# A shared expert moved ahead of a paired expert loop, and one of two sub-blocks fed to TensorE in two groups of 32 columns

## The chip, the cores and the metric

One core of a Trainium2 chip runs the whole program. The metric is the device time of one execution in microseconds (us); the figure to predict is the median. TensorE does the matrix products, VectorE, ScalarE and GpSimd the rest, and DMA queues move data; the hardware profiler recorded one execution, from which all rows below come.

## What is computed

One layer of an encoder over 2048 tokens of width 1024 in float32: a windowed attention and a pooling branch with a residual, then a mixture of experts with a residual, then an RMS norm. The part the change touches is the mixture:

```python
def swiglu(h, wg, wu, wd):
    return (jax.nn.silu(h @ wg) * (h @ wu)) @ wd
...
    def expert_block(args):
        tok, rw, e = args
        xs = hp[tok]
        y = swiglu(xs, w_gate_e[e], w_up_e[e], w_down_e[e])
        return (y.astype(jnp.float32) * rw[:, None]).astype(hf.dtype)
...
    shared = swiglu(hf, w_sh_gate, w_sh_up, w_sh_down)
    return (routed + shared).reshape(B, S, D)
```

The router takes for each token the sigmoid scores of 128 experts, keeps four of eight groups and in them eight experts, and scales their weights to a sum of 2.5. Every expert and the shared one have gate and up weights of 1024 x 256 and down weights of 256 x 1024, 1 MB each. The router's choice depends on the inputs, so how many tokens an expert gets is known only when the kernel runs. The shared expert takes all 2048 tokens.

## The kernel before

**Token tiles.** `tiles` runs `step(i)` for i from -2 to 17 on every engine: 16 tiles of 128 tokens through norm, input projection, attention, pooling, output projection, second norm and router, each engine handling several tiles in different stages of one step. A step stores the residual x1 (`acc_tab`) and the normed rows h2 (`h2_tab`) in DRAM; SP also stores a tile of zeros into the second half of `acc_tab` (semaphore z_acc). For each token GpSimd scatters eight records (token, weight) into a table `rec_tab` ordered by expert. In it the shared expert stands as the first expert, with all tokens at weight 1 (`shrec`, NSH = 32).

**Index work.** After the last tile VectorE counts each expert's tokens, rounds up to sub-blocks of 64 rows (SUB), and works out for each sub-block its expert, its place in the ring and how many weight loads must have landed. TensorE turns these columns into rows (line 1075), VectorE casts them into `tab`; GpSimd gathers the records, TensorE transposes them (line 1080), and `rec` holds the row numbers of the next units.

**The paired loop.** A unit is two sub-blocks of 64 rows that may belong to different experts. With 32 sub-blocks of the shared expert there were 174 units in the profiled run. Weights arrive in a ring of four slots, one expert each, loaded by SP in expert order (`gate_up`, `down` on the SP side), each when the unit that last used the slot is done. The first sub-block's products read their weights from the ring; for the second VectorE copies gate and up weights to `WBG` (line 886) and ScalarE the down weights to `WBD` (line 603). In one unit b of the loop TensorE does, in this order:

1. the gate and up product of unit b+1 (lines 1089 and 1090): eight k of 128 rows each, and in each k a product with 64 stationary columns for the first sub-block, output partitions 0 to 63, and one for the second, partitions 64 to 127, both 512 columns wide;
2. the first half of the down product of unit b (lines 1096 and 1097), two k;
3. eight transposes of the gathered rows of unit b+2 (line 977) and two of the hidden rows (line 1102);
4. the second half of the down product of unit b.

The stationary operand is a slice of the rows (`xTm`, `hT`), the moving one the weights. ScalarE does silu (594) and copies of transposes (597, 600), VectorE the gated product (892), its copy of transposes (889) and the scaling by routing weight and gate 2 (922), and GpSimd gathers the rows (477) and adds the results into `acc_tab` (511). The shape of a product on the array is in the trace as rows*columns, 128*64 here.

**End.** SP loads both halves of `acc_tab`; VectorE adds them, norms and stores.

Of the kernel before, what the change touches and what calls it, by code (L numbers as in the profile page):

```python
# [6 lines left out]
P = 128  # L7
# [29 lines left out]
NSH = T // SUB  # L37
NUNIT = 256
MAXU = (NSH + T * TOPK // SUB + E) // 2
# [9 lines left out]
            sub=4, after=4, start=4, half=1, shrec=2 * NT, inv=ROT, iotag=NG, tok=NT)  # L49
# [8 lines left out]
def constants():  # L58
# [20 lines left out]
    put("base", (t + 1) * T)  # L79
    sub = np.concatenate([2 * s, 2 * (s + P), 2 * s + 1, 2 * (s + P) + 1], 1)  # L80
    put("sub", sub)
    put("after", sub >= NSH)
    put("start", NSH * (sub >= NSH))
    put("half", (s >= SUB) * (T + P))
    shrec = np.zeros((P, NT, 2), np.int32)
    shrec[:, :, 0] = NT * s + np.arange(NT)[None, :]
    shrec[:, :, 1] = np.float32(1.0).view(np.int32)
    put("shrec", shrec.reshape(P, 2 * NT).view(np.float32))
# [27 lines left out]
def build(nc, A, out):  # L116
# [4 lines left out]
    with ctx:  # L121
# [8 lines left out]
        rec_tab = nc.dram_tensor("rec_tab", [(E + 1) * T + P, 2], i32).ap()  # L130
# [32 lines left out]
        def take(*shape):  # L163
# [80 lines left out]
            s_xin s_xres st_x1 st_h2 st_rec  # L244
            z_acc e_off e_row e_tab e_rec e_rf e_rT v_rec
# [14 lines left out]
        def ok(j):  # L260
            return not isinstance(j, int) or 0 <= j < NT

        def tiles(eng, step, chain=None, per_tile=0):

            for i in range(-2, 2):
                step(i)
            if chain:
                n0 = chain.n
            with eng.Fori(2, 14) as i:
                if chain:  # L270
                    chain.base, chain.n = eng.snap(i * per_tile + (n0 - 2 * per_tile)), 0
                step(i)
                if chain:
                    assert chain.n == per_tile, ("per tile", chain.n)
            if chain:
                chain.base, chain.n = 0, n0 + 12 * per_tile
            for i in range(14, 18):
                step(i)

# [18 lines left out]
        RF = arena[:, 42880:43392].bitcast(i32).rearrange("p (c r a) -> p c r a", c=4, a=2)  # L298
        RFf = arena[:, 42880:43392].rearrange("p (c r a) -> p c r a", c=4, a=2)
        RK = arena[:, 43392:43904].rearrange("p (k n r) -> p k n r", k=2, n=2)  # L300
        RI = over("RI", 2 * NUNIT, 43904, i32)
        RW = over("RW", NUNIT, 44416)
# [13 lines left out]
        def _(sp):  # L316
# [17 lines left out]
            halves = rec_tab[T:(E + 1) * T, :].rearrange("(e h t) a -> h e (t a)", e=E, h=2)  # L334
            for n in range(2):
                sp.dma_start(halves[n], pad_rec).then_inc(s["z_fill"], 16)
            sp.wait_ge(s["c_cst"], 16)
            sp.dma_start(rec_tab[0:T, :].rearrange("(p t) a -> p (t a)", p=P), C("shrec").bitcast(i32)).then_inc(s["z_fill"], 16)
            sp.dma_start(rec_tab[(E + 1) * T:(E + 1) * T + P, :].rearrange("(p t) a -> p (t a)", p=1), pad_rec[0:1, 0:2 * P]).then_inc(s["z_fill"], 16)
# [5 lines left out]
            sp.wait_ge(s["z_fill"], 64)  # L345
# [11 lines left out]
            def step(i):  # L357
# [15 lines left out]
            tiles(sp, step)  # L373

            def gate_up(l, e):
                at = (l + 3) % SLOTS * EW
# [5 lines left out]
            def down(l, e):  # L382
                at = (l + 3) % SLOTS * EW + GUW
# [3 lines left out]
            gate_up(0, None)  # L387
            down(0, None)
            sp.wait_ge(s["p_proj"], NT)
            sp.wait_ge(s["w_g"], 16)  # L390
            sp.wait_ge(s["w_u"], 16)
            gate_up(1, 0)
            sp.wait_ge(s["p_wo"], NT)
            for l in (2, 3):
                sp.wait_ge(s["w_g"], 16 * l)
                sp.wait_ge(s["w_u"], 16 * l)
                gate_up(l, l - 1)
                sp.wait_ge(s["w_d"], 16 * (l - 1))
                down(l - 1, l - 2)

            sp.wait_ge(s["w_g"], 64)
            sp.wait_ge(s["w_u"], 64)
            sp.wait_ge(s["gu_done"], NSH // 2)
            gate_up(4, 3)
            sp.wait_ge(s["w_d"], 48)
            down(3, 2)
            sp.wait_ge(s["e_tab"], 1)
            with sp.Fori(1, E // SLOTS) as q:
                for n in range(SLOTS):
                    e = sp.snap(q * SLOTS + n)  # L410
                    sp.wait_ge(s["w_g"], e * 16 + 16)
# [3 lines left out]
                    u = sp.value_load(tab[0:1, bass.ds(e + (6 * P - 3), 1)], min_val=1, max_val=MAXU)  # L415
                    sp.wait_ge(s["gu_done"], u)
                    settle(sp)
                    gate_up(n + 1, e)
                    sp.wait_ge(s["w_d"], e * 16)
                    settle(sp)  # L420
                    if n == 0:
                        w = sp.value_load(tab[0:1, bass.ds(e + (6 * P - 4), 1)], min_val=1, max_val=MAXU)
                    sp.wait_ge(s["y_done"], w)
                    settle(sp)
                    down(n, e - 1)
                    w = u
            sp.wait_ge(s["w_d"], E * 16)
            u = sp.value_load(tab[0:1, 6 * P + E - 4:6 * P + E - 3], min_val=1, max_val=MAXU)
            sp.wait_ge(s["y_done"], u)
            settle(sp)  # L430
            down(E, E - 1)
# [7 lines left out]
            nu = sp.value_load(nu_i[0:1, 0:1], min_val=NSH // 2 + 1, max_val=MAXU)  # L439
# [15 lines left out]
        def _(g):  # L455
# [16 lines left out]
            g.wait_ge(s["z_fill"], 64)  # L472
# [23 lines left out]
            g.wait_ge(s["z_acc"], 16 * NT)  # L496
            g.wait_ge(s["e_tab"], 1)
            nu = g.value_load(nu_i[0:1, 0:1], min_val=NSH // 2 + 1, max_val=MAXU)
# [20 lines left out]
        def _(act):  # L519
# [8 lines left out]
            def step(i):  # L528
# [24 lines left out]
                if ok(i - 1):  # L553
                    W8(act, "p_h2T", i)
                    A_(h2T[:, 0:4, :], B[2].rearrange("p (a b) -> p a b", a=4), ACT.Copy)
                    A_(h2T[:, 4:8, :], B[3].rearrange("p (a b) -> p a b", a=4), ACT.Copy).then_inc(s["a_h2T"], 1)
# [3 lines left out]
                if ok(i - 1):  # L560
                    W8(act, "p_rt", i)
# [24 lines left out]

            act.wait_ge(s["v_wo"], 1)
            tiles(act, step, ch, ACT_PER_TILE)

            act.wait_ge(s["e_tab"], 1)  # L590
            nu = act.value_load(nu_i[0:1, 0:1], min_val=NSH // 2 + 1, max_val=MAXU)
# [10 lines left out]
            def down_copy(src):  # L602
                nc.scalar.copy(WBD, src).then_inc(s["a_cd"], 1)  # L603
# [3 lines left out]
            act.wait_ge(s["w_d"], 16)  # L607
            down_copy(RING[:, 3 * EW + GUW:4 * EW])
# [6 lines left out]
            with act.Fori(0, MAXU // UNROLL) as q:  # L615
                with act.If(q * UNROLL < nu):
                    for n in range(UNROLL):
                        b = act.snap(q * UNROLL + n)
                        with act.If(b < nu):
                            at = act.value_load(tab[0:1, bass.ds(b + (2 * P + 1), 1)], min_val=0, max_val=(SLOTS - 1) * EW)  # L620
                            need = act.value_load(tab[0:1, bass.ds(b + (4 * P + 1), 1)], min_val=16, max_val=16 * (E + 1))
# [8 lines left out]
                            down_copy(RING[:, bass.ds(act.snap(at + GUW), HALF)])  # L630
# [16 lines left out]
        def _(v):  # L647
# [50 lines left out]
            v.wait_ge(s["z_fill"], 64)  # L698
# [17 lines left out]

            def step(i):
                if ok(i - 1):
# [54 lines left out]
                if ok(i):  # L773
# [4 lines left out]
                    last.then_inc(s["v_yT"], 1)  # L778
                if ok(i - 1):
# [23 lines left out]
                    settle(v)  # L803
                    link(V.max(m8, choice))
# [21 lines left out]
            tiles(v, step, ch, DVE_PER_TILE)  # L826

# [7 lines left out]
            link(V.tensor_tensor_scan(cum, sg[:, 0:E], nsub, float(NSH), ALU.mult, ALU.add))  # L835
# [6 lines left out]
            link(V.tensor_tensor(slot, slot, C("after"), ALU.add))  # L842
            link(V.tensor_tensor(first, first, C("start"), ALU.max))
            link(V.tensor_tensor(first, C("sub"), first, ALU.subtract))
            link(V.scalar_tensor_tensor(out=first, in0=slot, scalar=float(NSH), in1=first, op0=ALU.mult, op1=ALU.add))
            V.tensor_scalar(recb[:, :], first, float((E + 1) * NSH), None, ALU.min).then_inc(s["e_off"], 1)

            link(V.tensor_scalar(lc, slot, float(E), None, ALU.min))
            link(V.tensor_scalar(lq, lc, 0.25, 0.375, ALU.mult, ALU.add))
# [3 lines left out]
            V.tensor_scalar(offf[:, 0:4], lq, 3.0, float(EW), ALU.add, ALU.mult)  # L853
            V.tensor_scalar(offf[:, 4:6], lc[:, 2:4], 16.0, 16.0, ALU.mult, ALU.add)
            link(V.tensor_tensor(sg[:, 0:E], cum, nsub, ALU.subtract))
            link(V.tensor_tensor(sg[:, 0:E], sg[:, 0:E], ident, ALU.mult))
# [7 lines left out]
            V.tensor_copy(nu_i[:, :], units[0:1, :]).then_inc(s["e_off"], 1)  # L864
            v.wait_ge(s["e_row"], 1)
            V.tensor_copy(tab[:, 0:512], B[6][0:1, :])
            V.tensor_copy(tab[:, 512:512 + 3 * P], B[7][0:1, 0:3 * P]).then_inc(s["e_tab"], 1)

# [5 lines left out]
            last_.then_inc(s["e_rf"], 1)  # L874
            v.wait_ge(s["e_rT"], 1)
            V.tensor_copy(RI[:, 0:NUNIT], B[5][:, 0:NUNIT])
            V.tensor_scalar(RI[:, NUNIT:2 * NUNIT], B[5][:, 0:NUNIT], C("half"), None, ALU.add)
            link(V.tensor_copy(RW[:, :], B[5][:, NUNIT:2 * NUNIT]))
# [4 lines left out]
            nu = v.value_load(nu_i[0:1, 0:1], min_val=NSH // 2 + 1, max_val=MAXU)  # L883

            def gu_copy(n, src):
                V.tensor_copy(WBGf[n % 2], src).then_inc(s["v_cg"], 1)  # L886
# [8 lines left out]
            v.wait_ge(s["w_g"], 16)  # L895
            v.wait_ge(s["w_u"], 16)
            v.wait_ge(s["st_x1"], 16 * NT)
            gu_copy(0, RING[:, 3 * EW:3 * EW + GUW])
# [268 lines left out]
```

## Time and profile before

| | us |
|---|---|
| median of 2 runs | 3126.52 (3125.52 to 3127.51) |
| the profiled execution | 3141.75 |
| its span, first to last instruction | 3139.7 |
| TensorE products busy | 2849.2 (91%) |
| TensorE weight loads busy (beside products) | 1231.1 (39%) |
| VectorE busy | 1466.8 (47%) |
| ScalarE busy | 852.9 (27%) |
| GpSimd busy | 788.4 (25%) |

### The profile page before, as it was taken

The page shows a single profiled execution, that of the slowest core. Times are in us where ns is not written, and L with a number is a line of the kernel's source. Part 1 is how long each engine was busy: PE and PEld are TensorE (multiplying, and loading weights), DVE is VectorE, ACT ScalarE, POOL GpSimd, SP SyncE. Part 2 cuts the span into 40 slices and gives each one's busy share as a digit, 9 for nine tenths or more (in the row PEclk, how much of TensorE's full clock was granted, in tenths as well). Part 3 has the DMA queues.
Part 4 walks back from the last instruction along what each step waited for, and adds up shares of the span by engine and source line. Part 5 has one row for each costly group of instructions (what it writes and reads, how often), then busy time and mean ns, then how long its engine had stood idle before and what let it go on. Part 6 is the DMA issues. An engine that isn't in the chain of part 4 may idle for free.

```text
span 3139.7 us, 48012 instructions
## 1 busy us (share of the span) xinstructions
PE 2849.2 (91%) x13408; PEld 1231.1 (39%) x13409; DVE 1466.8 (47%) x2449; ACT 852.9 (27%) x1285; POOL 788.4 (25%) x493
## 2 busy tenths in 40 slices
PE   6789898898963999999999999999999999999990
PEld 2355545545541333333333333333333333333330
DVE  1146676666764444444444444444444444444345
ACT  0033333333320222222222222222222222222224
POOL 0000101111113333333332332333233333233220
PEclk9899999999986999999999999999999999999995
DMA  9611111211114347678999999899999996979958
GB/s 374 200 54 47 54 63 37 67 47 54 61 42 183 81 91 240 200 208 248 311 310 351 350 314 346 267 314 308 346 311 312 305 345 199 312 222 313 362 148 327
DMA packets 150957, 684.89 MB, mean 218 GB/s; under 512 B 26577, under 2 KB 27218, under 8 KB 101010
## 3 DMA queue, kind: packets, MB, share of 16 engines
q1 hardware_dynamic: 95730, 516.34, 41.3%
q0 software_dynamic: 55200, 168.21, 24.9%
q8 instruction: 14, 0.23, 0.0%
q14 instruction: 13, 0.11, 0.0%
HBM read 574.22 MB, written 128.07 MB: 224 GB/s over the span
## 4 chain that ended last, share of the span: by engine, by line
PE 61%; DMA 5%; DVE 1%; SPq 1%; issue 1%; POOL 0%; ACT 0%; DVEq 0%; POOLq 0%; ACTq 0%
PE PB L1089 36%; PE PB L1096 18%; PE PB L977 5%; DMA arena<-in_w_up_e 3%; PE PB L1102 1%; DMA arena<-acc_tab 1%; PE PB L1090 1%; DVE arena L954 0%; DVE arena L940 0%; SPq L415 0%; PE PB L1097 0%; DMA acc_tab<-arena,rec 0%; DMA arena<-h_tab,rec 0%; SPq L379 0%; SPq L446 0%
## 5 line engine op out<-in xcount | busy, mean ns | idle before, releaser
L1089 PE MATMUL PB<-arena 128*64 (+1 forms) x2800 | 1232.0, 593 | 2.1 <-issue 1.2
L1090 PE MATMUL PB<-arena 128*64 128x512 f32 x2800 | 1232.1, 593 | 0.0
L511 POOL DMA_INDIRECT acc_tab<-arena,rec x174 | 465.7, 2676 | 1361.8 <-DVE arena L922 1288.4
L1089 PEld LDWEIGHTS PB<-arena 128*64 128x64 f32 x2800 | 383.9, 137 | 802.4 <-issue 802.4
L1096 PE MATMUL PB<-arena 128*64 x1392 | 664.2, 599 | 0.0
L1097 PE MATMUL PB<-arena 128*64 128x512 f32 x1392 | 664.2, 599 | 0.0
L886 DVE COPY arena<-arena 128x4096 f32 (+1 forms) x177 | 405.0, 2288 | 59.9 <-DMA arena<-in_w_up_e 58.9
L922 DVE SCALAR_TENSOR_TENSOR arena<-PB,RW,G 128x512 f32<-128x512 f32 x348 | 245.3, 747 | 299.5 <-PE PB L1097 267.0
L1090 PEld LDWEIGHTS PB<-arena 128*64 128x64 f32 x2800 | 383.9, 137 | 0.0
L892 DVE TENSOR_TENSOR arena<-arena,PB 128x256 f32<-128x256 f32 x175 | 106.7, 610 | 543.4 <-ACT arena L594 541.3
L469 POOL DMA_INDIRECT rec_tab<-recs,posi x128 | 124.0, 969 | 849.3 <-DVE recs L758 809.4
L603 ACT COPY arena<-arena 128x2048 f32 (+1 forms) x175 | 330.9, 1891 | 0.0
L1096 PEld LDWEIGHTS PB<-arena 128*64 128x64 f32 x1392 | 176.6, 137 | 328.0 <-issue 328.0
L594 ACT ACTIVATE arena<-PB 128x256 f32<-128x256 f32 x175 | 67.1, 383 | 826.4 <-PE PB L1090 756.0
L977 PE MATMUL PB<-cst,arena 128*128 128x128 f32 x1664 | 231.4, 283 | 63.0 <-DVE arena L824 34.9
L1007 PE MATMUL PB<-arena 128*128 128x512 f32 (+1 forms) x768 | 280.2, 525 | 1.7 <-ACT arena L532 1.2
L977 PEld LDWEIGHTS PB<-cst,arena 128*128 128x128 f32 x1664 | 183.2, 142 | 217.8 <-issue 159.6
L889 DVE COPY arena<-PB 128x512 f32<-128x512 f32 x176 | 121.7, 691 | 291.8 <-PE PB L977 291.8
L1066 PE MATMUL PB<-arena 128*128 128x512 f32 x512 | 238.6, 627 | 9.6 <-ACT arena L571 6.8
L597 ACT ACTIVATE arena<-PB 128x512 f32<-128x512 f32 x176 | 105.4, 599 | 462.6 <-PE PB L977 462.6
L477 POOL DMA_INDIRECT arena<-h_tab,rec x178 | 187.8, 1055 | 62.5 <-issue 54.0
L1007 PEld LDWEIGHTS PB<-arena 128*128 128x128 f32 x768 | 145.2, 191 | 131.9 <-issue 120.6
(228 smaller groups left out, 1905.4 us busy)
## 6 DMA issues: line engine op xcount, KB each, us to landing
arena<-in_w_gate_e SPq DMA_DIRECT2D x128, 1024.0 KB
arena<-in_w_up_e SPq DMA_DIRECT2D x128, 1024.0 KB
arena<-in_w_down_e SPq DMA_DIRECT2D x128, 1024.0 KB
arena<-in_ada_w SPq DMA_DIRECT2D x12, 2048.0 KB, 13.0
arena<-in_x SPq DMA_DIRECT2D x32, 512.0 KB, 4.3
acc_tab<-arena SPq DMA_DIRECT2D x32, 512.0 KB, 5.0
arena<-acc_tab SPq DMA_DIRECT2D x6, 2048.0 KB, 22.2
h_tab<-arena SPq DMA_DIRECT2D x16, 512.0 KB, 2.9
```

The costliest lines, as they stand in the source:

```text
L477: g.indirect_dma_start(xg[n % AHEAD], None, h2_tab, bass.IndirectOffsetOnAxis(ap=rec[:, n % UNROLL, 0:1], axis=0), bounds_check=T - 1, oob ...
L511: g.indirect_dma_start(acc_tab, bass.IndirectOffsetOnAxis(ap=rec[:, n, 1:2], axis=0), ys[n % 2], None, compute_op=ALU.add).then_inc(s["add ...
L603: nc.scalar.copy(WBD, src).then_inc(s["a_cd"], 1)
L886: V.tensor_copy(WBGf[n % 2], src).then_inc(s["v_cg"], 1)
L922: last_ = V.scalar_tensor_tensor(out=ys[n % 2][:, c * 512:(c + 1) * 512], in0=B[4 + c], scalar=RW[:, bass.ds(b, 1)], in1=G2[:, c * 512:(c ...
L977: last = tr(B[banks[k // 4]][:, (k % 4) * P:(k % 4 + 1) * P], src[:, k * P:(k + 1) * P], ident)
L1007: last = mm(B[4 + n][:, 0:w], xT[:, k, :], w_in[:, k, n * 512:n * 512 + w], start=(k == 0), stop=(k == KD - 1))
L1066: last = mm(B[4 + n], mixT[:, k, :], w_out[:, k, n * 512:(n + 1) * 512], start=(k == 0), stop=(k == KD - 1))
L1089: mm(B[7][0:SUB, :], xTm[:, k, 0:SUB], wa(k), start=(k == 0), stop=(k == KD - 1))
L1090: last = mm(B[7][SUB:P, :], xTm[:, k, SUB:P], WBG[n % 2][:, k], start=(k == 0), stop=(k == KD - 1))
L1096: mm(B[4 + c][0:SUB, :], hT[:, k, 0:SUB], wa(k), start=(k == 0), stop=(k == 1))
L1097: last = mm(B[4 + c][SUB:P, :], hT[:, k, SUB:P], WBD[:, k * D + c * 512:k * D + (c + 1) * 512], start=(k == 0), stop=(k == 1))
```

## The change

**Shared expert.** It leaves the table of records, the counts and the loop (NSH, `shrec`, `after`, `start` go; MAXU is lower by 16; the ring's slot of expert e becomes e mod 4). Its weights are loaded into slot 3 before the token tiles begin, three SP issues ahead of `tiles(sp, step)`. In each tile SP now stores the transposed rows h2T in a new table `hT_tab` in place of the zeros, and ScalarE waits, before it overwrites h2T, for the store of the tile before. From the last token tiles on, `shared(j)` on each engine handles 16 tiles of 128 rows: SP loads the transposed rows into one of three buffers, TensorE does eight k of gate/up with all 128 stationary columns (half before and half after the two hidden transposes of the tile before) and the four down products of the tile before, ScalarE silu and a copy, VectorE the gated product and two products by gate 2, and SP stores the result as the second half of `acc_tab`. These tiles are written into the order of the router and index work: tile 0 after step 15 and tile 1 inside step 16 on TensorE, 2 and 3 before step 17, 4 to 7 before the row work, 8 to 11 before the transposes of the records, 12 to 15 after them. The first gathered rows are transposed between the hidden rows and the down product of tile 15. GpSimd waits for all 16 stores (sh_st) before its first scatter. The first units take weights from the ring through `tab` as all others.

**Second sub-block.** Its products are cut in two groups of 32 stationary columns, with output partitions 64 to 95 and 96 to 127, each over the same 512 moving columns as before.

```diff
-NSH = T // SUB
-MAXU = (NSH + T * TOPK // SUB + E) // 2
+RPE = T // SUB
+MINU = E // 2
+MAXU = (T * TOPK // SUB + E) // 2
...
-                if ok(i):
-                    sp.dma_start(acc_tab[bass.ds(i * P + (T + P), P), :], zeros).then_inc(s["z_acc"], 16)
+                if ok(i - 1):
+                    W8(sp, "a_h2T", i)
+                    sp.dma_start(rows(hT_tab, i - 1), h2T.rearrange("p k n -> p (k n)")).then_inc(s["st_hT"], 16)
...
+            gate_up(3, None)
+            down(3, None)
+            tiles(sp, step, between={NT - 1: first_rows})
             sp.wait_ge(s["p_proj"], NT)
-            gate_up(1, 0)
...
+            gate_up_after(0, 0)
+            down_after(0, 0)
+            for j in range(NT):
+                if j + 3 < NT:
+                    sp.wait_ge(s["sh_gu"], j + 1)
+                    shared_rows(j + 3)
...
+                sp.wait_ge(s["sh_ys"], j + 1)
+                W8(sp, "sh_st", 16 * j)
+                sp.dma_start(acc_tab[T + P + j * P:T + P + (j + 1) * P, :], yss[j % 2]).then_inc(s["sh_st"], 16)
+
+            sp.wait_ge(s["sh_y"], NT)
+            gate_up_after(3, 3)
+            down_after(3, 3)
...
-            g.wait_ge(s["z_acc"], 16 * NT)
+            g.wait_ge(s["sh_st"], 16 * NT)
...
                     W8(act, "p_h2T", i)
+                    W8(act, "st_hT", 16 * (i - 1))
...
+            def shared_gate_up(j, ks):
+                bank = B[0 if j % 2 else 7]
+                for k in ks:
+                    last = mm(bank, xTs[j % 3][:, k, :], gu_view(arena[:, 3 * EW + k * F:3 * EW + k * F + GUW]), start=(k == 0), stop=(k == KD - 1))
+                return last
...
+            def shared(j):
+                shared_begin(j)
+                if j:
+                    shared_hidden(j - 1)
+                shared_end(j)
+                if j:
+                    shared_down(j - 1)
...
-            tiles(pe, step)
-
+            tiles(pe, step, between={NT - 1: shared_first, NT: shared_next})
+
+            for j in range(4, 8):
+                shared(j)
             pe.wait_ge(s["e_off"], 2)
...
+            for j in range(12, NT):
+                shared(j)
+            shared_hidden(NT - 1)
+            pe.wait_ge(s["v_rec"], 1)
+            pe.wait_ge(s["xg_r0"], 16)
+            transposes((2, 3), xg[0], "xg_used")
+            shared_down(NT - 1)
...
                 for k in range(KD):
                     mm(B[7][0:SUB, :], xTm[:, k, 0:SUB], wa(k), start=(k == 0), stop=(k == KD - 1))
-                    last = mm(B[7][SUB:P, :], xTm[:, k, SUB:P], WBG[n % 2][:, k], start=(k == 0), stop=(k == KD - 1))
+                    for r in (slice(SUB, 96), slice(96, P)):
+                        last = mm(B[7][r, :], xTm[:, k, r], WBG[n % 2][:, k], start=(k == 0), stop=(k == KD - 1), tile_position=(0, r.start))
                 last.then_inc(s["gu_done"], 1)
...
                 for k in range(2):
                     mm(B[4 + c][0:SUB, :], hT[:, k, 0:SUB], wa(k), start=(k == 0), stop=(k == 1))
-                    last = mm(B[4 + c][SUB:P, :], hT[:, k, SUB:P], WBD[:, k * D + c * 512:k * D + (c + 1) * 512], start=(k == 0), stop=(k == 1))
+                    for r in (slice(SUB, 96), slice(96, P)):
+                        last = mm(B[4 + c][r, :], hT[:, k, r], WBD[:, k * D + c * 512:k * D + (c + 1) * 512], start=(k == 0), stop=(k == 1), tile_position=(0, r.start))
                 return last
```

## Rows read from the trace of the kernel before

**Rows 1.** Table of stretches: stretch, its length, busy (count) per engine, clock, DMA share, GB/s.

```profile
150.00:170.00 20.00, 9.66 (x43) 6.65 (x43) 4.25 (x11) 6.89 (x16) 0.00 (x0) 0.78 0.07 18
928.00:1000.00 72.00, 12.38 (x52) 9.07 (x52) 37.59 (x114) 5.67 (x10) 28.49 (x25) 0.58 0.53 196
1012.00:2852.00 1840.00, 1839.67 (x9124) 697.50 (x9126) 783.90 (x943) 495.00 (x628) 584.14 (x313) 1.00 0.84 272
2852.00:2992.00 140.00, 130.80 (x642) 49.26 (x640) 55.18 (x67) 34.69 (x44) 36.49 (x23) 0.96 1.01 351
```

**Rows 2.** TensorE's timeline within a unit: start us, duration us, line, tile, count.

```profile
1802.71 0.59 PE L1097 MATMUL PB<-arena 128*64 128x512 f32 x1
...
1803.99 0.59 PE L1096 MATMUL PB<-arena 128*64 x1
1804.00 0.59 PE L1097 MATMUL PB<-arena 128*64 128x512 f32 x1
1804.52 1.09 PE L977 MATMUL PB<-cst,arena 128*128 128x128 f32 x8
1805.45 0.38 PE L1102 MATMUL PB<-cst,arena 128*128 128x128 f32 x2
1805.76 0.64 PE L1096 MATMUL PB<-arena 128*64 x1
...
1806.24 0.59 PE L1096 MATMUL PB<-arena 128*64 x1
...
1816.21 1.09 PE L977 MATMUL PB<-cst,arena 128*128 128x128 f32 x8
```

**Rows 3.** The page's costliest groups: count, busy us, mean ns of one, idle before.

```profile
L1089 PE MATMUL PB<-arena 128*64 (+1 forms) x2800 | 1232.0, 593 | 2.1 <-issue 1.2
L1089 PEld LDWEIGHTS PB<-arena 128*64 128x64 f32 x2800 | 383.9, 137 | 802.4 <-issue 802.4
L1096 PE MATMUL PB<-arena 128*64 x1392 | 664.2, 599 | 0.0
L886 DVE COPY arena<-arena 128x4096 f32 (+1 forms) x177 | 405.0, 2288 | 59.9 <-DMA arena<-in_w_up_e 58.9
L922 DVE SCALAR_TENSOR_TENSOR arena<-PB,RW,G 128x512 f32<-128x512 f32 x348 | 245.3, 747 | 299.5 <-PE PB L1097 267.0
L892 DVE TENSOR_TENSOR arena<-arena,PB 128x256 f32<-128x256 f32 x175 | 106.7, 610 | 543.4 <-ACT arena L594 541.3
L603 ACT COPY arena<-arena 128x2048 f32 (+1 forms) x175 | 330.9, 1891 | 0.0
L594 ACT ACTIVATE arena<-PB 128x256 f32<-128x256 f32 x175 | 67.1, 383 | 826.4 <-PE PB L1090 756.0
```

**Rows 4.** TensorE's timeline from the last token tile to the loop, and the loop's end.

```profile
924.65 3.17 PE L1066 MATMUL PB<-arena 128*128 128x512 f32 x7
...
939.08 1.97 PE L977 MATMUL PB<-cst,arena 128*128 128x128 f32 x8 [11.15 <-DVE arena L740]
...
1000.66 1.08 PE L1089 MATMUL PB<-arena 128*64 128x512 f32 x1 [0.88 <-DVE arena L889]
...
1009.46 1.09 PE L977 MATMUL PB<-cst,arena 128*128 128x128 f32 x8
...
1012.33 0.64 PE L1089 MATMUL PB<-arena 128*64 x1 [1.25 <-issue]
...
3057.57 0.59 PE L1096 MATMUL PB<-arena 128*64 x1
```

**Rows 5.** TensorE's timeline in a token tile: the scores, and the attention product.

```profile
600.22 1.59 PE L991 MATMUL PB<-arena 64*64 64x128 f32 x32
601.75 0.23 PE L998 MATMUL PB<-c 128*128 128x128 bf16 x1
...
626.87 1.09 PE L1043 MATMUL PB<-arena 128*64 128x256 f32 x8 [1.32 <-issue]
627.89 0.38 PE L1047 MATMUL PB<-arena,poolw 128*128 128x128 f32 x1
```

More of the change, by code:

```diff
@@ L48 @@
 COLS = dict(ident=P, band0=NPG * P, band=NPG * P, bandp=NPG * P, tri=P, iota=P, base=P,
-            sub=4, after=4, start=4, half=1, shrec=2 * NT, inv=ROT, iotag=NG, tok=NT)
+            sub=4, half=1, inv=ROT, iotag=NG, tok=NT)
 AT = {}
@@ L261, in ok, with tiles @@
             return not isinstance(j, int) or 0 <= j < NT
-        def tiles(eng, step, chain=None, per_tile=0):
+        def tiles(eng, step, chain=None, per_tile=0, between={}):
             for i in range(-2, 2):
@@ L278, in tiles @@
                 step(i)
+                if i in between:
+                    between[i]()
         def rows(table, i):
@@ L778, in step @@
                     last.then_inc(s["v_yT"], 1)
+                if last_tile:
+                    shared_gated(0)
+                    shared(1)
                 if ok(i - 1):
@@ L803, in step @@
                     settle(v)
+                    if last_tile:
+                        shared(2)
                     link(V.max(m8, choice))
@@ L824, in step @@
                     V.tensor_tensor(xn, xn, B1, ALU.add).then_inc(s["v_xn"], 1)
-            tiles(v, step, ch, DVE_PER_TILE)
+            tiles(v, step, ch, DVE_PER_TILE, between={NT: lambda: shared(3)})
+            shared(4)
             cnt, nsub, cum, le = rk, scores, choice, repl
@@ L893, in gated @@
                                 B[7][:, F:2 * F].rearrange("t (p k) -> t p k", k=2), ALU.mult).then_inc(s["h_ready"], 1)
[L895 to L898, printed above, removed]
+            shared(12)
+            gu_copy(0, 0)
+            for j in range(13, NT):
+                shared(j)
             v.wait_ge(s["xg_used"], 1)
             rows_lower()
-            gu_copy(1, RING[:, 3 * EW:3 * EW + GUW])
+            v.wait_ge(s["sh_hp"], NT)
+            gu_copy(1, 1)
+            shared_out(NT - 1)
             v.wait_ge(s["eg_done"], 1)
@@ L1025, in step @@
                 if ok(i - 1):
+                    if isinstance(i, int) and i == NT:
+                        shared(1)
                     W8(pe, "a_h2T", i)
@@ L1070, in _ @@
             pe.wait_ge(s["c_win"], 16)
-            tiles(pe, step)
+            tiles(pe, step, between={NT - 1: shared_first, NT: shared_next})
+            for j in range(4, 8):
+                shared(j)
             pe.wait_ge(s["e_off"], 2)
             for c in range(NTABS):
-                row = mm(B[6 + c // 4][0:1, (c % 4) * P:(c % 4 + 1) * P], offf[:, c:c + 1], ident, start=True, stop=True)
+                row = mm(B[6 if c < 4 else 3][0:1, (c % 4) * P:(c % 4 + 1) * P], offf[:, c:c + 1], ident, start=True, stop=True)
             row.then_inc(s["e_row"], 1)
+            for j in range(8, 12):
+                shared(j)
             pe.wait_ge(s["e_rf"], 1)
```

259 lines of the change are left out of this document (159 added, 100 removed).

## The prediction

> **What bounds the kernel now.** I read the page first, for the busy shares and the costliest groups, then a table of stretches, then TensorE's timeline inside one unit of the paired loop and between the token tiles and that loop. The reader is to see four things.
>
> First, the paired loop is the program: TensorE is busy for 1839.67 of the 1840 us from 1012 to 2852 at the full clock of 2.4 GHz (1.00 in the table), and afterwards starves a little (130.80 of 140) where the DMA share is 1.01 [rows 1]. Second, a unit lasts 11.69 us, from the transposes at 1804.52 to those at 1816.21 [rows 2]. Each fp32 product runs as two passes (175 gate/up sets of eight products give 2800 passes per sub-block, 174 down sets give 1392 [rows 3]), a pass of 512 columns takes 0.43 us (1802.71 to 1804.00 is three), and the passes of the two sub-blocks start within 0.01 us of each other [rows 2]. So 48 passes cost the time of 24. Third, VectorE (2288 + 2 x 747 + 610 ns and one copy of some 0.7, about 5 us a unit) and ScalarE (1891 + 383 ns and two more short copies, about 3.3 us) fit in 11.69 us with room [rows 3]. Fourth, between the last token tile (seven passes from 924.65, the last streamed by 927.65) and the first gate/up at 1000.66 [rows 4], TensorE is busy for 12.4 of 72 us, at a granted clock of 0.58, and waits for VectorE and DMA otherwise [rows 1].
>
> **The change, part by part.** The loop's bodies run from 1012.33 to the last pass, 3057.57 plus 0.43 [rows 4]: 2045.7 us for 174 units, of which 174 x 11.69 = 2034.1 is the unit and 11.6 is starving.
>
> *The shared expert leaves the loop.* Its 32 sub-blocks of 64 rows were 16 units, so 158 units stay. It comes back as 16 tiles of 128 rows with full-width products: 24 passes and 2 transposes each. A full-width pass also takes 0.43 us (seven merged in 3.17 us, of which the last is 0.59: six steps of 0.43 [rows 4]), so a tile is 24 x 0.4287 + 2 x 0.11 = 10.51 us, and 16 are 168.2 us. A unit of the shared expert was 11.69, so the array time saved is only 16 x 1.18 = 19 us; the rest of the gain is that these tiles fill the hole before 1000.66. TensorE from 927.65: 168.2, plus 4.6 waiting for the last tile's h2 (shared tile 0 ends at 934.5, the transposes can start at 939.08 [rows 4]), plus 6 to 12 for the router, table and row work that is there today (12.4 at today's clock of 0.58, about half at full clock [rows 1]), plus 1.4 for the last hidden rows' trip through ScalarE and VectorE. The first gate/up starts near 1109 instead of 1000.66, and the first body near 1119 instead of 1012.33, since today's first set runs partly at a lower clock (8.8 us) and waits 1.25 us after it [rows 4]. I take **+107 us**; bounds 105 (no waits) and 125 (each of the 16 tiles waits 1 us for a hand-over of 0.38 + 0.61 us [rows 3]).
>
> What this hides costs nothing: VectorE's 16 x (0.61 + 2 x 0.75) = 34 us [rows 3] and its index work (37.6 us busy today [rows 1]) lie beside 180 us of TensorE; the router chain comes about 10 us later, beside shared products. The shared weights (three SP issues of 1 MB) move ahead of the tile loop's input rows in SP's queue; the DMA share from 150 to 170 is 0.07 [rows 1], so they have landed before anyone waits; without that cover they cost some 9 us at the 351 GB/s of the busiest stretch [rows 1]. The zero fill of the second accumulator half becomes a store of h2T of the same 512 KB in each tile; ScalarE's new wait for that store is for one issued a whole token tile earlier, and behind it wait the h2T copy and TensorE's router product. Row loads and result stores of the shared tiles, 1 MB per 10.5 us, go beside the loads of experts 0 to 2. Expert 3's weights are asked for only when the shared tiles are done; they are wanted some units later, and GpSimd's first scatter waits for the last result store, which has a whole unit. If all of this were exposed I would not get over 20 us.
>
> *The second sub-block in two groups of 32 columns.* Call the groups A (columns 0 to 63), B and C (64 to 95, 96 to 127). The order is A, B, C for each k. No row shows a 32-wide group beside a 64-wide one, so this is bounded from both sides.
>
> What rows do show is how TensorE treats tiles. In the attention product (line 1043) the order in the program is two instructions for the one column half, then two for the other, yet 8 passes of 256 columns (0.214 us each) start at 626.87 and are followed at 627.89, that is four passes' time and 0.16: an instruction for another tile of the same shape overtakes waiting ones. The scores (line 991) do 32 passes of 128 columns (0.107 us) in 1.53 us, less than 16 x 0.107 = 1.71, so more than two tiles ran at once there [rows 5]. But between shapes it is different: from 128*64 to 128*128 the last pass starts at 1804.00 and the next shape at 1804.52, 0.09 after the 0.43 it streams; back again, two transposes of 0.11 (eight take 0.93 with the change before them) start at 1805.45 and the next shape at 1805.76, again 0.09; and the first pass after each change takes 0.48, not 0.43 [rows 2]. So a change of shape ends all overlap, its weights aren't loaded ahead, and it costs 0.09 + 0.05 = **0.14 us**. Check: 24 x 0.4287 + 10 x 0.11 + 2 x 0.14 = 11.67, against 11.69.
>
> If 64 and 32 columns are two shapes in this sense, A runs alone for two passes, then B and C together for two. A unit then has 48 passes' time (20.58), ten transposes 1.10, and 25 changes (A to BC and back for each of twelve k, one more for the transposes): 25 x 0.14 = 3.50. Sum **25.2 us**, against 11.69. The first gate/up takes 16 us for 7. If the changes of width cost nothing but the turn, the unit is 20.58 + 1.10 + 0.28 = 22.0. If a change waits for the recorded end of a pass (0.59 less 0.43) and then for a whole weight load of 0.13 (weight loads of 128*64 average 137 ns [rows 3]), it costs 0.29 and the unit 28.9. I take 25.2, because the same step is seen twice in each unit. TensorE would wait for nothing else, and the 11.6 us of starving go, as an expert's 3 MB gets twice the time.
>
> On the one side stands the Trainium skill, "TensorEngine Tiling (Array Packing)", section "Key Properties": changing the tiling mode, not just the tile, drains TensorE, and its list has 128x64 and 128x32 as two modes; by it the sum is the one below. By that rule, the trace agrees as far as it goes: the 0.09 us gaps. On the other, "TensorE: Matmul & The Clock Gate", section "The mechanism", addresses the array in 32-column strips by mask and lets different positions overlap; by it the sum is that of the first rival.
>
> **Sum.** The profiled run took 3141.75 us (span 3139.7); the median is 3126.52, 15 lower, and I carry that over. 3126.5 + 107 + 9 (first gate/up) + 158 x 25.18 (3978.4) - 2045.7 = **5175 us**. The two bounds of the change give 3126.5 + 107 + 7 + 158 x 21.96 - 2045.7 = 4665 and 3126.5 + 107 + 11 + 158 x 28.9 - 2045.7 = 5765; the start's bound adds 18 at most.
>
> **The rivals.**
> 1. *Three groups at once; the width is no change of shape.* Groups that touch different columns don't conflict, and [rows 5] show more than two tiles at once. Then the unit stays 11.69 and the starving stays: 3126.5 + 107 + 158 x 11.69 + 11.6 - 2045.7 = **3046 us**, 2.6% faster. It decides as soon as one pass of B starts within a pass of A. The second page named above speaks for it. Against it: every change of shape in the trace drained, though each there was between tiles that share columns, so the rows can't exclude it. Chance 0.14, of which 0.03 that waits in the 16 shared tiles keep it above 3064.
> 2. *Two at once.* The array takes any two groups: three passes' time per pair, unit 12 x 1.286 + 1.38 = 16.8, 3126.5 + 107 + 4 + 2654 - 2045.7 = 3846 us. The scores speak against it [rows 5]. 0.02.
> 3. *B and C one after the other too*, since they read the same columns of weights: unit 72 x 0.4287 + 1.10 + 3.50 = 35.5, about 6810 us. Same-shape overlap speaks against it. 0.02.
> 4. *The clock falls to 1.2 GHz* in the loop, as half of the columns idle: passes of 0.86 us, unit near 47 us, about 8640 us. The clock was 0.96 where TensorE was busy for 130.80 of 140 us [rows 1]; streaming would be 82% of the new unit. 0.02.
>
> **How the numbers follow.** The likeliest is taking turns, 0.80, at 5175 us with 4660 to 5765 as its range; that already holds 8 in 10, so the other cases stay out of the range. A difference under 2% is about what can't be told from no change. Faster by over 2%: 0.11 (rival 1). Within 2%: 0.03. Slower: 0.80 + 0.06 = 0.86.
>
> **What would show it.** First set of shared products from 927.7 on without holes over 5 us, and the first gate/up near 1109; 158 units. In a unit: passes of A with none of B or C beside them, B and C within 0.01 us of each other, steps of 0.48 and 0.52 us by turns, 2.0 us per k in the gate/up. TensorE busy throughout, no idle for weights. I am wrong if a pass of 32 columns starts while one of 64 streams, if a change costs far from 0.14 us, or if the granted clock in the loop falls below 1.00.

## The result and the profile after

The changed kernel takes 5154.72 us (median of two runs, 5153.79 to 5155.65) where the kernel before takes 3126.52: a ratio of 1.648, with an interval of 1.645 to 1.651. The forecast was 5175, in a range of 4660 to 5765.

First the page of the changed kernel: busy time and share of each engine, the granted clock of TensorE in 40 slices, the instruction queue (packets, MB, share), and the costliest groups.

```profile
PE 4943.8 (96%) x16704; PEld 1342.3 (26%) x16705; DVE 1430.5 (28%) x2398; ACT 818.1 (16%) x1255; POOL 818.4 (16%) x461
...
PEclk9899999999999999999999999999999999999996
...
q8 instruction: 19, 0.31, 0.0%
...
L1220 PE MATMUL PB<-arena 128*64 x2544 | 1363.9, 618 | 1.1 <-DVE arena L961 1.1
L1222 PE MATMUL PB<-arena 128*32 128x512 f32 x5088 | 1338.3, 605 | 0.0
...
L1228 PE MATMUL PB<-arena 128*64 x1264 | 677.7, 618 | 0.0
L1230 PE MATMUL PB<-arena 128*32 128x512 f32 x2528 | 664.9, 605 | 0.0
```

The gate/up passes of the first sub-block (L1220) and of the two groups of the second (L1222) are busy for 1364 and 1338 us. In the kernel before, the passes of the two sub-blocks lay on top of each other and the group of one of them had 1232 us in all [rows 3]; here the two lines add up. Their idle time is 1.1 and 0.0 us: nothing is waited for. VectorE is busy for 28% of the span and ScalarE for 16%, so the loop is TensorE's alone.

One unit on TensorE (start us, duration us, line, tile, count; passes that overlap or follow at once are merged into one line):

```profile
3005.25 1.07 PE L1228 MATMUL PB<-arena 128*64 x2
3006.25 1.05 PE L1230 MATMUL PB<-arena 128*32 128x512 f32 x4
3007.23 1.07 PE L1228 MATMUL PB<-arena 128*64 x2
3008.23 1.05 PE L1230 MATMUL PB<-arena 128*32 128x512 f32 x4
3009.22 1.09 PE L1094 MATMUL PB<-cst,arena 128*128 128x128 f32 x8
3010.15 0.38 PE L1235 MATMUL PB<-cst,arena 128*128 128x128 f32 x2
3010.46 1.07 PE L1228 MATMUL PB<-arena 128*64 x2
```

Two passes of the 64-wide group run alone, then four of the 32-wide ones in the time of two, then the next two of the 64-wide: 1.00 and 0.98 us by turns, 1.98 us for a k. [rows 2] had the same k of both sub-blocks in 0.86 us. The distances between single records, which the rows above merge, say where it goes. Within a turn of the 64-wide group the second pass starts 0.480 us after the first, and the first 32-wide pass 0.523 after that, which is 0.429 of streaming (the step between passes of one width, as in [rows 2]) and 0.094 of nothing. Within a turn of the 32-wide groups the step is 0.453, and the two groups start 0.007 us apart; the next 64-wide pass starts 0.522 after the later of them. From 1130 to 5050 us no pass of one width starts less than 0.521 us after the last one of the other.

From the last token tile to the loop, also on TensorE:

```profile
909.13 7.03 PE L1048 MATMUL PB<-arena 128*128 128x512 f32 x16
...
920.26 1.97 PE L1094 MATMUL PB<-cst,arena 128*128 128x128 f32 x8 [3.99 <-DVE arena L798]
...
1091.11 1.07 PE L1220 MATMUL PB<-arena 128*64 x2
...
1106.99 1.09 PE L1094 MATMUL PB<-cst,arena 128*128 128x128 f32 x8
...
1109.71 1.07 PE L1220 MATMUL PB<-arena 128*64 x2 [1.09 <-DVE arena L961]
...
5068.55 1.05 PE L1230 MATMUL PB<-arena 128*32 128x512 f32 x4
```

The shared tiles begin at 909.13, where the last token tile ends, have one hole of 3.99 us and a small one of 0.38, and the first gate/up of the loop follows at 1091.11. The first body starts at 1109.71, where it was 1012.33 [rows 4]. From there to the end of the last pass at 5069.4 (its start, 5069.0, plus 0.43) are 3959.7 us, 158 units of 25.06; before, it was 2045.7 for 174.

The table of stretches (length, busy and count of each engine, clock, DMA share, GB/s):

```profile
928.00:1110.00 182.00, 180.43 (x493) 78.78 (x492) 61.21 (x145) 18.21 (x39) 26.91 (x25) 1.00 0.45 162
1130.00:5050.00 3920.00, 3920.00 (x12830) 797.80 (x12828) 796.44 (x941) 494.43 (x627) 673.58 (x313) 1.00 0.44 137
150.00:170.00 20.00, 10.12 (x35) 5.87 (x33) 3.84 (x11) 6.50 (x15) 0.00 (x0) 0.86 0.34 140
```

Where [rows 1] had TensorE busy for 12.38 of 72 us at a clock of 0.58, it is busy for 180.43 of 182 at 1.00. In the loop it never waits, at 2.4 GHz throughout, with a DMA share of 0.44.

### The profile page after: what moved, and what is told of

It reads as the page before. It is cut to its first block, busy times and chain, and to the rows that moved or that the text cites. A ratio compares the mean times of both kernels' runs of the same rounds, so it can differ in the third digit from the quotient of the medians.

```text
span 5151.8 us, 53361 instructions
## 1 busy us (share of the span) xinstructions
PE 4943.8 (96%) x16704; PEld 1342.3 (26%) x16705; DVE 1430.5 (28%) x2398; ACT 818.1 (16%) x1255; POOL 818.4 (16%) x461
## 4 chain that ended last, share of the span: by engine, by line
PE 91%; DVE 5%; DMA 2%; ACT 1%; issue 1%; SPq 0%; DVEq 0%; ACTq 0%; POOLq 0%
PE PB L1220 25%; PE PB L1222 24%; PE PB L1228 12%; PE PB L1230 12%; PE PB L1124 6%; PE PB L1094 4%; PE PB L1048 2%; PE PB L1040 1%; PE PB L1071 1%; DMA arena<-in_ada_b 1%; PE PB L1185 1%; PE PB L1235 1%; PE PB L1151 1%; PE PB L1108 1%; DMA arena<-acc_tab 0%
## 5 line engine op out<-in xcount | busy, mean ns | idle before, releaser
L1220 PE MATMUL PB<-arena 128*64 x2544 | 1363.9, 618 | 1.1 <-DVE arena L961 1.1
L1222 PE MATMUL PB<-arena 128*32 128x512 f32 x5088 | 1338.3, 605 | 0.0
L528 POOL DMA_INDIRECT acc_tab<-arena,rec x158 | 515.6, 3263 | 3250.6 <-DVE arena L994 3080.6
L1228 PE MATMUL PB<-arena 128*64 x1264 | 677.7, 618 | 0.0
L1230 PE MATMUL PB<-arena 128*32 128x512 f32 x2528 | 664.9, 605 | 0.0
L964 DVE TENSOR_TENSOR arena<-arena,PB 128x256 f32<-128x256 f32 x159 | 96.3, 606 | 1802.8 <-ACT arena L632 1802.7
L1220 PEld LDWEIGHTS PB<-arena 128*64 128x64 f32 x2544 | 243.1, 134 | 1066.7 <-issue 1066.7
L1222 PEld LDWEIGHTS PB<-arena 128*32 128x32 f32 x5088 | 183.5, 108 | 1032.0 <-issue 1032.0
L958 DVE COPY arena<-arena 128x4096 f32 x161 | 369.5, 2295 | 147.5 <-issue 76.8
L994 DVE SCALAR_TENSOR_TENSOR arena<-PB,RW,G 128x512 f32<-128x512 f32 x316 | 222.7, 746 | 601.0 <-PE PB L1230 601.0
L641 ACT COPY arena<-arena 128x2048 f32 x159 | 300.5, 1890 | 0.7 <-issue 0.7
L1094 PE MATMUL PB<-cst,arena 128*128 128x128 f32 x1536 | 213.5, 283 | 66.1 <-DVE arena L887 53.2
L1228 PEld LDWEIGHTS PB<-arena 128*64 128x64 f32 x1264 | 120.8, 134 | 423.8 <-issue 423.8
L1230 PEld LDWEIGHTS PB<-arena 128*32 128x32 f32 x2528 | 91.2, 108 | 512.8 <-issue 512.8
L494 POOL DMA_INDIRECT arena<-h_tab,rec x162 | 167.9, 1037 | 158.3 <-issue 94.3
```

The source lines that it names most:

```text
L494: g.indirect_dma_start(xg[n % AHEAD], None, h2_tab, bass.IndirectOffsetOnAxis(ap=rec[:, n % UNROLL, 0:1], axis=0), bounds_check=T - 1, oob ...
L528: g.indirect_dma_start(acc_tab, bass.IndirectOffsetOnAxis(ap=rec[:, n, 1:2], axis=0), ys[n % 2], None, compute_op=ALU.add).then_inc(s["add ...
L641: nc.scalar.copy(WBD, RING[:, bass.ds(act.snap(at + GUW), HALF)]).then_inc(s["a_cd"], 1)
L958: V.tensor_copy(WBGf[n % 2], RING[:, bass.ds(at, GUW)]).then_inc(s["v_cg"], 1)
L994: last_ = V.scalar_tensor_tensor(out=ys[n % 2][:, c * 512:(c + 1) * 512], in0=B[4 + c], scalar=RW[:, bass.ds(b, 1)], in1=G2[:, c * 512:(c ...
L1094: last = tr(B[banks[k // 4]][:, (k % 4) * P:(k % 4 + 1) * P], src[:, k * P:(k + 1) * P], ident)
```

## The experiments

My theory was that the 64-wide and the 32-wide groups take turns because TensorE drains at each change of tile shape, and that all of the loss lies there. The rivals: that the *number* of groups costs (three matmuls where two were), that the change of shape costs only its gaps and not the overlap, and that the move of the shared expert has a part in the loss. The chips of these runs give the kernel before 3147 to 3148 us, 21 more than the first; so I go by the ratios.

**The parts apart: e1_shared_only and e2_split_only.** The first keeps the shared tiles and puts the second sub-block back into one group of 64 columns (in the down products the same):

```diff
-                    for r in (slice(SUB, 96), slice(96, P)):
-                        last = mm(B[7][r, :], xTm[:, k, r], WBG[n % 2][:, k], ..., tile_position=(0, r.start))
+                    last = mm(B[7][SUB:P, :], xTm[:, k, SUB:P], WBG[n % 2][:, k], ...)
```

> The changed kernel with the second sub-block's products as one group of 64 columns again; only the shared expert's move is left. Theory (two additive parts): a unit is back at 11.69 us, 158 of them, with the loop's first body some 100 us later after the last token tile than in the kernel before (193.7 less 8.9 of the first split gate/up, against 84.7), and the starving on weights near the loop's end is back: 3126.5 + 100 - 16 x 11.69 = 3040 us, ratio to before 0.972. Rival A (the slowdown is partly the shared tiles' own, for instance through the ring's new start): the unit stays above 12 us and the time above 3200. Rival B (the shared tiles gain nothing because they only move work): 3110 to 3140.

The second is the kernel before with the two `for r` loops alone.

> The kernel before with only the second sub-block split in two groups of 32 columns. Theory (a change of shape drains the array, 25.07 us a unit as in the changed kernel): 3126.5 + 9 + 174 x 25.07 - 2045.7 = 5452 us, ratio 1.744. Rival (the parts interact, the split costs less where the shared tiles are in the loop): the 16 shared units differ from the others, and the total is off by over 50 us.

Measured: e2 takes 5469.4 us, ratio 1.737 (1.733 to 1.741), and all its 174 units have the same form and last 25.06 us. It adds 2322 us to the kernel before, where I had expected 2325. So the split alone makes the loss, and it makes it in the kernel before as in the changed one. TensorE in e2:

```profile
2000.92 0.38 PE L1104 MATMUL PB<-cst,arena 128*128 128x128 f32 x2
2001.23 1.07 PE L1097 MATMUL PB<-arena 128*64 x2
2002.23 1.05 PE L1099 MATMUL PB<-arena 128*32 128x512 f32 x4
2003.21 1.07 PE L1097 MATMUL PB<-arena 128*64 x2
```

e1 missed its expectation: 3149.3 us, ratio 1.001 (0.998 to 1.003), where I had expected 0.972. The move of the shared expert takes 16 units out of the loop and gives no time. The median unit is 11.69 us, and the stretch ahead of the loop is 106 us longer than before, where I had expected some 100. But ten units, from transposes to transposes, last 12.8 to 24.3 us, and all units together take 85.6 us more than 158 medians; in the kernel before it was 10.6. TensorE stands still for 64 of the 85.6 us, and the rest are passes at a lower granted clock behind the holes (0.98 over the whole loop). Where I speak of starving, in the expectations too, it is this sum. One of those holes in e1, on TensorE:

```profile
2868.35 1.09 PE L1094 MATMUL PB<-cst,arena 128*128 128x128 f32 x8
2879.86 0.69 PE L1233 MATMUL PB<-cst,arena 128*128 128x128 f32 x2 [10.42 <-DVE arena L964]
```

And the weight loads that SP issues in e1 around it (start, duration, queue, line, out<-in):

```profile
2859.99 0.33 SPq L386 DMA_DIRECT2D arena<-in_w_down_e  x1
2863.91 0.34 SPq L380 DMA_DIRECT2D arena<-in_w_gate_e  x1
2864.35 0.38 SPq L381 DMA_DIRECT2D arena<-in_w_up_e  x1
2884.28 0.33 SPq L386 DMA_DIRECT2D arena<-in_w_down_e  x1
2885.77 0.33 SPq L380 DMA_DIRECT2D arena<-in_w_gate_e  x1
```

The chain of work behind that hole (start, duration, what):

```profile
2864.35 12.44 DMA arena<-in_w_up_e
...
2879.22 0.60 DVE arena L964
```

The hole ends with the up weights asked for at 2864.35: VectorE's copy of them starts at 2877.01, after 15.35 us of waiting for this load, and the gated product L964, which TensorE needs, comes behind the copy. So that load was asked for too late. And while TensorE waits SP asks for nothing: after down, gate and up the next issue comes 20 us later, once TensorE goes on. The changed kernel does not only renumber the ring's slots. It also rewrites the order on SP: behind the gate and up of expert e comes the down of the same expert, which waits for `y_done` of the last unit that used the slot (expert e - 4), and that product comes behind the gate/up of the next unit; the kernel before put the down of e - 1 there, which waits for a product one expert further back. Every gate and up behind it in SP's queue waits with it. My part-by-part list had gone over SP's queue in the start only.

**The load order: e6_down_behind and e8_before_own_down.** e6 is e1 with the order of the kernel before, the down of e - 1 behind the gate and up of e (in short form):

```diff
                     gate_up(n, e)
-                    sp.wait_ge(s["w_d"], e * 16 + 16)
-                    sp.wait_ge(s["y_done"], u)
-                    down(n, e)
+                    sp.wait_ge(s["w_d"], e * 16)
+                    sp.wait_ge(s["y_done"], w)
+                    down((n - 1) % SLOTS, e - 1)
```

> The kernel with the shared expert moved and no split (e1), and SP's order of weight loads as in the kernel before: the down weights of an expert are asked for after the gate and up weights of the next one, so that the wait for the last unit's y_done holds nothing up. In e1 the units starved for 85.6 us in all, in the kernel before for 10.6. Theory (SP's wait for y_done ahead of the next expert's gate and up weights causes it): starving falls back to 10 to 20 us and the time by some 70 us, ratio to before 0.975 to 0.98. Rival (the head start is missing: the kernel before fills four slots during 16 shared units): starving stays above 60 us and the ratio near 1.00.

e8 is the kernel before with nothing but the other order:

```diff
-                    sp.wait_ge(s["w_d"], e * 16)
+                    sp.wait_ge(s["w_d"], e * 16 + 16)
...
-                    sp.wait_ge(s["y_done"], w)
-                    down(n, e - 1)
+                    sp.wait_ge(s["y_done"], u)
+                    down(n + 1, e)
```

> The kernel before, with only SP's order of loads changed to the changed kernel's: each expert's down weights right behind its own gate and up weights, with the wait for y_done of the slot's last unit between. Theory (this order causes the starving): starving rises from 10.6 to some 80 us, time 70 us above the kernel before, ratio 1.02. Rival (missing head start): no change, ratio 1.00.

Measured: e6 takes 3077.55 us, ratio **0.977** (0.975 to 0.979), faster than both kernels; e8 3227.7, ratio 1.025 (1.024 to 1.027). Here w is the last unit of expert e - 5, where u is that of e - 4. The same piece of the loop in the table of stretches, for e1:

```profile
1300.00:2852.00 1552.00, 1520.19 (x7484) 574.82 (x7482) 652.38 (x775) 406.86 (x516) 495.14 (x258) 0.99 0.89 291
```

For e6:

```profile
1300.00:2852.00 1552.00, 1552.00 (x7700) 589.32 (x7696) 673.74 (x797) 417.68 (x530) 554.80 (x266) 1.00 0.90 300
```

For e8:

```profile
1300.00:2852.00 1552.00, 1513.60 (x7453) 571.34 (x7450) 638.14 (x769) 404.10 (x513) 431.79 (x258) 0.99 0.89 288
```

TensorE (the first figure after the length) stands still for 32 of the 1552 us in e1 and for 38 in e8, and for none in e6, at practically the same DMA share. Over the whole loop the units take 85.6 us above their median in e1, 12.4 in e6, 10.6 in the kernel before and 91.9 in e8; the standing still in them is 64, 11, 11 and 71 us. So the load order costs some 75 to 80 us, and it costs them in either kernel. The move of the shared expert by itself is worth 2.3%; the changed kernel's own load order takes that back. In the changed kernel none of it shows, since a unit of 25 us gives the loads twice the time.

**More groups of one width: e3_four_groups and e7_first_32.** e3 cuts the first sub-block into 32 columns too. It does not compute the same: rows 32 to 63 of the first sub-block are multiplied by the second sub-block's weights, with counts and sizes unchanged.

```diff
-                    mm(B[7][0:SUB, :], xTm[:, k, 0:SUB], wa(k), ...)
-                    for r in (slice(SUB, 96), slice(96, P)):
+                    mm(B[7][0:32, :], xTm[:, k, 0:32], wa(k), ...)
+                    for r in (slice(32, SUB), slice(SUB, 96), slice(96, P)):
```

> The changed kernel with the first sub-block split as well, so that all four groups have 32 columns and no width alternates. [...] Theory (only the change between 64 and 32 columns costs): four groups run side by side, a unit is 11.7 to 12.0 us (eight loads and products per 0.857 us at most a little slower to issue), total near 3040 to 3090 us. Rival 1 (groups cost by their number, or instructions for waiting groups block the queue): four groups per k take at least what three do, 5155 us or more. Rival 2 (two groups at once are the most): 48 passes in pairs as seen with three groups, a unit of 21.9 us, about 4650 us.

e7 has the first of these lines and not the second, so each k has three groups of 32, and rows 32 to 63 of the first sub-block are left out.

> The changed kernel with the first sub-block's group cut to 32 columns: rows 32 to 63 of it are left out. The number of products and the order of the three groups are those of the changed kernel; no width alternates. Theory (the change between 64 and 32 columns costs): units of 11.7 us as in e1, total within 40 us of e1's, ratio 1.00, and no stall at every eighth unit as with four groups, since the program is no longer than the changed kernel's. Rival (the cost comes with the third group or with the queue): unit near 25 us, total 5150.

Measured: e7 takes 3139.9 us, ratio 0.998 (0.997 to 1.000), with a unit of 11.67 us and 85.7 us above that in all, just as e1. TensorE in e7:

```profile
2000.02 0.59 PE L1220 MATMUL PB<-arena 128*32 x1
2000.03 0.60 PE L1222 MATMUL PB<-arena 128*32 128x512 f32 x2
2000.45 0.59 PE L1220 MATMUL PB<-arena 128*32 x1
```

Three groups start within 0.01 us, and the next three 0.43 later. Between the changed kernel and e7 only the width of the first group differs, 64 against 32 columns, and that is a ratio of 1.648 against 0.998. It is the mixing of widths and not the number of groups.

e3 has a median unit of 11.68 us, four groups side by side, which was the point in dispute. But it takes 3292.0 us, ratio 1.044 (1.042 to 1.047), where I had expected 3040 to 3090. Every eighth unit (8, 16, 24 up to 144) lasts some 20 us. Its instruction queue on the page (packets, MB, share of the DMA engines):

```profile
q8 instruction: 202, 3.31, 0.4%
```

And TensorE in e3 at unit 8:

```profile
1230.42 0.59 PE L1228 MATMUL PB<-arena 128*32 x1
1230.42 0.60 PE L1230 MATMUL PB<-arena 128*32 128x512 f32 x3
1237.03 1.06 PE L1220 MATMUL PB<-arena 128*32 x1 [6.00 <-DVE arena L958]
1237.04 1.07 PE L1222 MATMUL PB<-arena 128*32 128x512 f32 x3
1237.88 1.06 PE L1220 MATMUL PB<-arena 128*32 x1
...
1242.01 0.59 PE L1220 MATMUL PB<-arena 128*32 x1
1242.02 0.60 PE L1222 MATMUL PB<-arena 128*32 128x512 f32 x3
```

The loop's body holds eight units, and the hole comes once in each of its rounds. The records put it down to VectorE's copy, but the instruction queue, 19 packets in the changed kernel and 14 in the one before, now has 202: 12 of them fall between 1200 and 1330 us, where e1 has none, and 3 between 1228 and 1238. After 6 us of standing still the passes take 0.85 us instead of 0.43, which is the 1.2 GHz level, until 1242.01: 6.2 us of nothing and 2.4 of slower passes, 8.6 a round and some 155 in the 18 rounds that show it. Against e1, which shares the rest, e3 is 143 us longer. What ties the hole to program code is that the packets and the holes come in the same run, the only one with four groups for each k; I did not run a shorter body, so that cause is likely and not shown.

**Fewer changes: e4_one_turn and e5_split_down.** e4 keeps all groups and widths and changes the order: the first group for all k, then the two others for all k.

```diff
                 for k in range(KD):
                     mm(B[7][0:SUB, :], xTm[:, k, 0:SUB], wa(k), ...)
+                for k in range(KD):
                     for r in (slice(SUB, 96), slice(96, P)):
```

> The changed kernel with the order inside a product changed: first the 64-column group for all k, then both 32-column groups for all k. The same passes, but 7 changes of shape in a unit instead of 25. Theory (a change costs 0.09 us of drain plus 0.05 before a 64-wide and 0.025 before a 32-wide group, and the turn itself costs the lost overlap): gate/up 13.98 us, each half of down 3.69, transposes 1.23, unit 22.6 us, total 5154.7 - 158 x 2.47 - 2 = 4763 us. Rival (the change costs nothing, each pass of a split group is slower in itself): the unit stays at 25.07 and the total at 5155.

e5 has the split in the down products only; gate/up is one group of 64 again, as in e1.

> The changed kernel with the split in two groups of 32 columns in the down products only, not in gate and up: four of the twelve k of a unit. Theory (a price per k, whatever the product): unit 11.69 + 4 x (1.98 - 0.857) = 16.2 us, little starving, e1's time less its 86 us and plus 158 x 4.5: 3149 - 86 + 709 = 3770 us, ratio 1.20. Rival (the price hangs on the length of the accumulation or on waits around gate and up): the unit is off by over 0.5 us.

Measured: e4 takes 4795.0 us, ratio 1.523 (1.519 to 1.527), with a unit of 22.65 us, as expected (4763 over 3126.5 is 1.523); e5 3797.8, ratio 1.206 (1.202 to 1.210), with a unit of 16.05. TensorE in e4:

```profile
2005.49 7.06 PE L1223 MATMUL PB<-arena 128*32 128x512 f32 x32
2012.48 1.93 PE L1229 MATMUL PB<-arena 128*64 x4
2014.34 1.91 PE L1232 MATMUL PB<-arena 128*32 128x512 f32 x8
2016.18 1.09 PE L1094 MATMUL PB<-cst,arena 128*128 128x128 f32 x8
```

The 32 passes of the two narrow groups take 6.99 us, sixteen steps. With 7 changes instead of 25 a unit is 2.41 us shorter, 0.134 for each change saved. The 10.3 us of lost overlap stay. That says less than it seems: in this order a 32-wide pass would have to overtake up to fifteen waiting 64-wide ones to run beside the first of them, and no row shows whether TensorE could do that even for one width. e5 shows the same piece by piece: for 8 of the 24 steps the overlap goes (8 x 0.43 = 3.4 us) and seven more changes come (0.9), and the unit is 4.36 longer. Its total is 28 us above what I expected, mainly because it starved for 40.4 us (29 of standing still), in six units, all of them among the ten late ones of e1. The load order explains that in kind; I did not try e5 with the other order.

## Why the prediction came out

It was right in its mechanism. That it came within 20 us in 5155 is partly luck: the units were put 18.7 us too high and the start 18.5, and a base 16.2 us too low took most of one of them back.

- **TensorE drains between widths.** The step on which all hung holds: a 64-wide pass has no 32-wide one beside it, also where they use different columns of the array, which the rows of before could not show. By the page "TensorEngine Tiling (Array Packing)" of the Trainium skill, section "Key Properties", changing the mode drains the engine; the trace agrees, and puts 0.094 us on it. The run that shows it is the mixed width is e7: with the first group at 32 columns too the passes overlap again.
- **Price of a change.** I took 0.14 us, the same both ways. It is 0.094 and then 0.051 of a late first step ahead of a 64-wide group, as in [rows 2], but only 0.025 ahead of a 32-wide one (0.119). By these a unit is 20.58 + 12 x 0.264 + 1.10 + 0.14 = 24.99, measured 25.06, forecast 25.18; the 0.007 us by which the second 32-wide group starts late, twelve times, is the rest. Over 158 units this term was 18.7 us too high.
- **Lost overlap against changes.** Of the 13.37 us that a unit gained, 24 x 0.4287 = 10.3 are the passes that no longer share time and 3.1 the changes; e4, with 7 changes instead of 25, takes away 2.4 us of the second part and none of the first.
- **Start.** The first gate/up comes 182.0 us after the last token tile (forecast 181.4), the first body 115.9 us later by that measure than before (forecast 107 + 9). The holes, the clock and the hidden shared weights came as written. But the token tiles themselves ended at 909.13 and not at 927.65, 18.5 us earlier. I see nothing in the change that makes them faster: with the same code for them they ended at 929.7 in e1, and over the profiles of e1 to e8 between 929.3 and 956.0. I had taken 927.65 for a fixed point.
- **The 15 us carried over.** I took the distance between the profiled run and the median of before as something to be kept. The profiled run of after is 0.9 us *below* its median. So the start was too late by 18.5 us and the base too low by 16.2 (15.2 + 0.9), and the two nearly cancelled. Perhaps the 15 us of before were those same token tiles in one execution; the runs behind the median have no trace, so this isn't shown.
- **Starving.** In the changed kernel it went, as said. In rival 1 it was mis-sized: I let 11.6 us of starving stay, and with three groups at once it is 85.7, as e7 shows. e7 is that rival made real, by equal widths: a ratio of 0.998, which for before's 3126.5 is 3121 us and not 3046, no change instead of 2.6% faster. With the load order of before, as in e6, a ratio of 0.977 is 3053. The step that failed is in the part on the shared expert: "Expert 3's weights are asked for only when the shared tiles are done" costed the first load, and I did not compare what each further load waits for.
- **Rivals 2 to 4** all fall. Two at once: no 32-wide pass in the loop starts less than 0.521 us after a 64-wide one, which streams for 0.429. B and C in series: they start 0.007 us apart. The clock: 1.00 in the whole loop.

Open remains why the token tiles, which are the same code in the changed kernel and in e6, end at 909 us in the one profile and at 956 in the other. The granted clock is near in both, 0.97 and 0.95 from 200 to 900 us, and the kernel before had 0.97 as well.

## What to carry to other kernels

Before you split or narrow a matmul that shares TensorE's array, ask whether its neighbours keep the same tile shape: one narrow group among wide ones costs the whole overlap first (10.3 of 13.4 us here) and the changes second (3.1 us), and fewer turns mended only the second (e4). When a change renumbers a ring of buffers, write down for each load in the queue which product it waits for, before and after; here one load put a place ahead cost 75 to 80 us and ate the gain of the other half of the change. A stage that a slow loop hides is not thereby fine: e1 shows it as soon as the loop is fast again.

## What the runs showed of the hardware

- A change between 64-wide and 32-wide tiles costs 0.119 us towards the narrow and 0.145 towards the wide side; that is 0.094 of standing still each time and a first step longer by 0.025 and 0.051. I had not expected the second part to depend on the width.
- Groups of one width ran side by side in each of the numbers tried: two of 64 (11.69 us a unit), three of 32 (11.67), four of 32 (11.68).
- Four groups per k in a loop of eight units went with 202 packets on the instruction queue and one hole of 6 us in each round, and the 1.2 GHz level for 5 us after it. Three groups per k, 53361 instructions in all, had neither; four have 60977.
